# Output projection by tokens, a new order at the start of the up product, and earlier first loads of the down product

## The chip, the cores and the metric

The kernel runs on one NeuronCore of a Trainium2 chip. The metric is the device time of one execution in microseconds (us), as the median of the runs. The engines have instruction queues of their own and meet only in semaphores: TensorE (PE: matmuls and transposes), VectorE (DVE), ScalarE (ACT), GpSimd (POOL) and SyncE (SP), whose queue here issues nearly all DMAs.

## The reference, cut to what matters

```python
h = x + concat(y_attention, y_hgrn2) @ w_out        # 1024 tokens x 1024, w_out 1024 x 1024
u = rmsnorm(h, mlp_norm_w)
h = h + square(relu(u @ w_up)) @ w_down             # w_up 1024 x 4096, w_down 4096 x 1024
```

All in float32. What stands ahead of these lines (norm, input projection, neighbourhood attention, HGRN2) is not touched.

## The kernel before, in words

**Precision.** Each float32 operand is split into a rounded part (hi, by ACT or POOL) and a rest (lo, a subtraction by DVE or POOL), and each product is three matmuls: hi*hi, hi*lo, lo*hi.

**Output projection.** `w_out` comes in 8 tiles of 128 rows (tiles 32 to 39 of `TILES`), which POOL splits into a ring of 4 slots (lines 798 and 801). Two tiles make a block (`FBLK = 2`), and there are four blocks (`OUT_BLOCKS`). For each block PE computes 16 products (8 token tiles times two column halves) of 6 matmuls each (lines 2026 to 2030), DVE adds each from its bank to `resid` (line 1620), and the next block does the same again. In the last block, once both halves of a token tile are added, ACT takes the sum of squares and the inverse root (`rms`, lines 873 to 876) and DVE writes the normalised tokens (line 1295).

**Sets.** The up and down products use Strassen's scheme: 7 products in place of 8, numbered 1 to 7. For the up product the moving operand is one of 7 sets of turned (transposed) tokens, kept for the whole stage; each set has 4 parts, so there are 28 (`g`). A part is four PE transposes into a bank (`turn_set`, line 1785), a copy by ACT (hi, line 1066), and a subtraction by DVE (lo, line 1304); then its bank is free again. Sets 7 and 5 need sums of tokens that POOL makes (lines 841 and 843), set 6 four sums and set 4 four more by DVE (lines 1645 and 1649), which overwrite tokens.

**Up product.** It has 16 blocks (`UPS`, index j) of 7 products of 12 matmuls (lines 2069 to 2073). `UP_SEQ` is the order of the 112 products; those of blocks 0 and 1 are interleaved and `SET_IN` says which of them have set parts turned between their matmuls. Weight n of that order passes POOL (a sum, for products 7, 5, 6 and 3), ACT (hi, line 1076) and POOL (lo, line 834). The results are put together by DVE (`up_results`, lines 1658 to 1664, `up_last_results`), squared by ACT (`square`, lines 1099 and 1102), summed by DVE (`act_sums`) and stored to DRAM. ACT, DVE and POOL run in an order written out by hand, so each waiting instruction holds up all that follows it on its engine.

**Down product.** It has 56 slots m of 24 matmuls (lines 2100 to 2104). ACT takes the hi part of its weights (line 1113) and of its activations (line 1122); the lo parts are DVE's (line 1711) and POOL's (line 854). The first data (1 MB twice for each pair of weight tiles, and four times 0.5 MB of activations) is loaded after the stores of block 14 (`load_down`, `load_acts`), and ACT takes it in up block 15 at steps k = 3 and after.

## Time and profile before

| | |
|---|---|
| Median of 3 runs | 1390.39 us (1389.7 to 1391.82) |
| The profiled execution | 1393.67 us, span 1391.9 us |
| PE busy | 1307.8 us, 94% of the span |
| DVE, ACT, POOL busy | 875.7, 579.1, 575.5 us |
| Chain that ended last | PE 80%, DVE 10%, ACT 4% |

The span runs from the first to the last record; the execution's own time is 1.8 us longer. Times in rows are microseconds from the start of the span. A busy PE can still run at the lower of two clocks: the column PEclk is the granted share of full speed. "idle before" is the time an engine stood before an instruction, and the name behind it what ended that.

### The profile page before, as it was taken

The numbers are of one execution on the slowest core, as the hardware profiler recorded it, in microseconds if no ns is written. First come the engines' busy times: TensorE is split into PE (matmuls) and PEld (weight loads), VectorE is DVE, ScalarE is ACT, GpSimd is POOL, SyncE is SP. The second block draws the span as 40 slices with busy tenths as digits, with TensorE's granted clock in tenths as the row PEclk, the third lists the DMA queues.
The fourth block names the chain that finished last, engine by engine and source line by source line (L and its number), as shares of the span: only waits on it lengthen the run. The fifth ranks groups of instructions, "written<-read, shape, count | busy, mean of one in ns | idle before, by whom it ended". The sixth has DMA issues, their size and how long they took to land.

```text
span 1391.9 us, 18095 instructions
## 1 busy us (share of the span) xinstructions
PE 1307.8 (94%) x6624; PEld 1099.5 (79%) x6624; DVE 875.7 (63%) x1202; ACT 579.1 (42%) x1034; POOL 575.5 (41%) x324
## 2 busy tenths in 40 slices
PE   4998999999999999899986799999999999999998
PEld 4976777898888888787864688888887788888887
DVE  5445677651687786956674434344443788888885
ACT  5235656444344453232053445544443433333341
POOL 5232211123322132213246467777773544445452
PEclk9999999999999999999997899999999999999999
DMA  8341232222111010114140344454446934353433
GB/s 240 116 114 31 71 91 75 73 72 81 31 31 31 16 31 31 59 49 157 56 151 9 110 148 143 144 159 152 144 144 229 360 128 175 106 212 107 151 91 136
DMA packets 138533, 154.93 MB, mean 111 GB/s; under 512 B 11472, under 2 KB 97744, under 8 KB 138448
## 3 DMA queue, kind: packets, MB, share of 16 engines
q1 hardware_dynamic: 132976, 147.04, 32.6%
q10 hardware_dynamic: 5472, 6.75, 1.4%
q8 instruction: 54, 0.88, 0.3%
q14 instruction: 31, 0.25, 0.1%
HBM read 109.72 MB, written 44.04 MB: 110 GB/s over the span
## 4 chain that ended last, share of the span: by engine, by line
PE 80%; DVE 10%; ACT 4%; issue 3%; POOL 2%; DMA 1%; ACTq 0%; SPq 0%; DVEq 0%; POOLq 0%
PE bank L2100 7%; PE bank L2103 7%; PE bank L2104 7%; PE bank L2069 6%; PE bank L2072 6%; PE bank L2073 6%; PE bank L1820 5%; PE bank L1824 5%; PE bank L1823 5%; PE bank L1904 4%; PE bank L2026 2%; PE bank L2030 2%; PE bank L2029 2%; PE bank L1807 2%; PE bank L1810 2%
## 5 line engine op out<-in xcount | busy, mean ns | idle before, releaser
L798 POOL TENSOR_TENSOR w_hi<-stage,one_col 128x1024 fp32r<-128x1024 f32 x40 | 78.8, 1971 | 498.1 <-PE bank L1820 344.5
L854 POOL TENSOR_TENSOR a_split<-a_raw,a_split 128x1024 fp32r<-128x1024 f32 x56 | 148.1, 2663 | 170.6 <-ACT a_split L1122 170.6
L2069 PE MATMUL bank<-set,w_hi 128*128 128x512 f32 x448 | 180.7, 403 | 12.9 <-DVE u L1660 6.5
L2100 PE MATMUL bank<-w_hi,a_split 128*128 128x512 f32 x448 | 175.2, 391 | 5.4 <-issue 5.4
L2072 PE MATMUL bank<-set,w_hi 128*128 128x512 f32 x448 | 178.5, 398 | 0.0
L2073 PE MATMUL bank<-set,w_lo 128*128 128x512 f32 x448 | 178.3, 398 | 0.0
L2103 PE MATMUL bank<-w_lo,a_split 128*128 128x512 f32 x448 | 175.0, 391 | 0.0
L2104 PE MATMUL bank<-w_hi,a_split 128*128 128x512 f32 x448 | 174.9, 390 | 0.0
L1820 PE MATMUL bank<-uT_hi,w_hi 128*128 128x512 f32 x384 | 160.4, 418 | 6.4 <-DVE h_gate L1352 6.4
L1824 PE MATMUL bank<-uT_hi,w_lo 128*128 128x512 f32 x384 | 151.3, 394 | 0.0
L1823 PE MATMUL bank<-uT_lo,w_hi 128*128 128x512 f32 x384 | 150.7, 393 | 0.0
L2069 PEld LDWEIGHTS bank<-set,w_hi 128*128 128x128 f32 x448 | 85.9, 192 | 33.1 <-issue 14.3
L834 POOL TENSOR_TENSOR w_lo<-stage,w_hi 128x512 fp32r<-128x512 f32 x56 | 75.6, 1352 | 80.5 <-ACT w_hi L1076 80.5
L2100 PEld LDWEIGHTS bank<-w_hi,a_split 128*128 128x128 f32 x448 | 84.5, 189 | 23.9 <-issue 6.2
L801 POOL TENSOR_TENSOR w_lo<-stage,w_hi 128x1024 fp32r<-128x1024 f32 x40 | 101.6, 2540 | 3.1
L2073 PEld LDWEIGHTS bank<-set,w_lo 128*128 128x128 f32 x448 | 85.6, 191 | 19.7
L2072 PEld LDWEIGHTS bank<-set,w_hi 128*128 128x128 f32 x448 | 85.8, 191 | 18.6
L2104 PEld LDWEIGHTS bank<-w_hi,a_split 128*128 128x128 f32 x448 | 84.5, 189 | 17.7
L2103 PEld LDWEIGHTS bank<-w_lo,a_split 128*128 128x128 f32 x448 | 84.5, 189 | 17.4
L834 POOL TENSOR_TENSOR w_lo<-raw_b,w_hi 128x512 fp32r<-128x512 f32 x56 | 74.4, 1329 | 42.7 <-ACT w_hi L1076 42.7
L1711 DVE TENSOR_TENSOR w_lo<-raw,w_hi 128x1024 fp32r<-128x1024 f32 x35 | 74.4, 2131 | 26.4 <-ACT w_hi L1113 26.4
L1820 PEld LDWEIGHTS bank<-uT_hi,w_hi 128*128 128x128 f32 x384 | 72.9, 190 | 21.7 <-DVE h_gate L1352 7.2
(183 smaller groups left out, 2869.9 us busy)
## 6 DMA issues: line engine op xcount, KB each, us to landing
a_dram<-abuf SPq DMA_DIRECT2D x112, 256.0 KB, 2.1
a_raw<-a_dram SPq DMA_DIRECT2D x56, 512.0 KB, 3.7
stage<-in_w_in SPq DMA_DIRECT2D x32, 512.0 KB, 4.1
raw<-in_w_down SPq DMA_DIRECT2D x10, 1024.0 KB, 8.5
stage<-in_w_up SPq DMA_DIRECT2D x16, 512.0 KB, 5.0
raw_b<-in_w_up SPq DMA_DIRECT2D x16, 512.0 KB, 5.1
x_tok<-in_x SPq DMA_DIRECT2D x8, 512.0 KB, 5.5
v_dram<-vs ACTq DMA_DIRECT2D x32, 128.0 KB, 1.8
```

The costliest lines, as they stand in the source:

```text
L801: pool.tensor_tensor(w_lo[:, i, :], stage[:, i % STAGE, :], w_hi[:, i, :].bitcast(F32), ALU.subtract).then_inc(w_split, 1)
L834: pool.tensor_tensor(ring_part(w_lo, n), here, ring_part(w_hi, n).bitcast(F32), ALU.subtract).then_inc(x_lo, 1)
L854: pool.tensor_tensor(a_split[:, m % 4, 1, :], a_raw[:, m % 4, :], a_split[:, m % 4, 0, :].bitcast(F32), ALU.subtract).then_inc(b_lo, 1)
L1820: first = pe.matmul(b[:, :], w[0], u[0], start=k == 0, stop=False)
L1823: pe.matmul(b[:, :], w[0], u[1], start=False, stop=False)
L1824: ins = pe.matmul(b[:, :], w[1], u[0], start=False, stop=k == KT - 1)
L2069: first = pe.matmul(dst, w[0], u[0], start=k == 0 and p in (1, 5, 6, 7), stop=False, skip_group_check=True)
L2072: pe.matmul(dst, w[0], u[1], start=False, stop=False, skip_group_check=True)
L2073: ins = pe.matmul(dst, w[1], u[0], start=False, stop=k == 3, skip_group_check=True)
L2100: first = pe.matmul(dst, a[0], w[0], start=start, stop=False, skip_group_check=True)
L2103: pe.matmul(dst, a[0], w[1], start=False, stop=False, skip_group_check=True)
L2104: ins = pe.matmul(dst, a[1], w[0], start=False, stop=q == 1 and k == 1, skip_group_check=True)
```

## The change

- **Output projection.** Blocks 2 and 3 become one round: each of the 16 products has 12 matmuls and is added once. The split tiles 38 and 39 go to a place of their own (`w_late`), and the mixer's split parts have four places (`mixed`) in place of two. The token tiles so come to their end one after the other over the whole of the last round.
- **Start of the up product.** ACT splits weights 0 to 3 ahead of the norms, set parts 0 to 7 are turned after products 9 to 12 of the round, and (1, 6) moves ahead of (0, 4) and (0, 3). The other 20 parts are placed one by one (`TURNED_AT`), with other banks for the last two. ACT takes weights 6 to 13 in pairs between the set parts. POOL makes two sums before the last token sums. DVE takes set parts 16 to 19 between its two groups of four sums, and does the results of block 1 before the activation sums of block 0, for which one result has another place (`act_part`).
- **Start of the down product.** In SP's order the first half of the first weights and the first four activation loads come ahead of the stores of block 14, the second half after three of these stores. `a_raw` and `raw_2` change places, ACT and DVE take the first weight and ACT the first two activations earlier in block 15.

```diff
-UP_SEQ = [(0, 1), (0, 2), (1, 1), (1, 2), (0, 7), (1, 7), (0, 5), (1, 5), (0, 6), (0, 4), (0, 3), (1, 6), (1, 4), (1, 3)]
+UP_SEQ = [(0, 1), (0, 2), (1, 1), (1, 2), (0, 7), (1, 7), (0, 5), (1, 5), (0, 6), (1, 6), (0, 4), (0, 3), (1, 4), (1, 3)]
...
-SET_BANK = (4, 5, 6, 7, 4, 5, 6, 7, 1, 5, 3, 7, 1, 5, 0, 1, 5, 0, 1, 5, 0, 1, 5, 0, 5, 0, 5, 0)
-SET_IN = {(1, 1): 2, (1, 2): 3, (1, 7): 4, (0, 5): 5, (1, 5): 6}
+SET_BANK = (4, 5, 6, 7, 4, 5, 6, 7, 1, 5, 3, 7, 1, 5, 0, 1, 5, 0, 1, 5, 0, 1, 5, 0, 5, 0, 0, 1)
+TURNED_AT = {(1, 1, 2): 8, (1, 1, 3): 9, (1, 2, 0): 10, (1, 2, 1): 11, (1, 2, 2): 12, (1, 2, 3): 13, (0, 7, 0): 14,
+             (0, 7, 1): 15, (0, 7, 2): 16, (0, 7, 3): 17, (1, 7, 0): 18, (1, 7, 1): 19, (0, 5, 2): 20, (0, 5, 3): 21,
+             (1, 5, 0): 22, (1, 5, 1): 23, (0, 6, 0): 24, (0, 6, 1): 25, (1, 6, 0): 26, (1, 6, 2): 27}
...
+        mixed = [acts[:, 0], over("mixed1", [P, 2, FBLK, S], F32R, first + 49152),
+                 over("mixed2", [P, 2, FBLK, S], F32R, first + 16384), acts[:, 1]]
+        w_late = over("w_late", [P, FBLK, 2, D], F32R, first + 32768)
...
-        a_raw = over("a_raw", [P, 4, D], F32, work + 81920)
+        a_raw = over("a_raw", [P, 4, 2, D], F32, work)[:, :, :, HALF:D]
-        raw_2 = over("raw_2", [P, 4, D], F32, work)
+        raw_2 = over("raw_2", [P, 4, D], F32, work + 81920)
...
+        def act_part(j, i):
+
+            return u_tok[:, TT - 1, HALF:D] if (j, i) == (1, A22) else abuf[:, i, :]
...
-                return w_used, N_TILES - 2 if n < 4 else N_TILES
+                return w_used, N_TILES - 4 if n < 4 else N_TILES
...
-                        sp.wait_ge(down_done, 16 * (OUT_BLOCKS - 1))
+                        sp.wait_ge(down_done, 16)
...
-                        sp.wait_ge(up_used, UP_AT[(UPS - 1, 4)] + 1)
+                        sp.wait_ge(up_used, UP_AT[(UPS - 1, 5)] + 1)
...
-                    sp.wait_ge(up_used, UP_AT[(UPS - 1, 5)] + 1)
+                    sp.wait_ge(y_turned, 28)
...
-            sp.wait_ge(proj_done, len(UNITS))
...
+                if j == UPS - 2:
+                    load_down(0, (0,))
+                    for m in range(4):
+                        load_acts(m)
+                for i in (A22, A11, A12):
                     store_acts(j, i)
-            load_down(0)
+                if j == UPS - 2:
+                    load_down(0, (1,))
+                for i in (S1, S3, S2, S4):
+                    store_acts(j, i)
             load_down(1)
-            for m in range(4):
-                load_acts(m)
...
-            split_turns(1, N_TILES // RING)
+            split_turns(1, N_TILES // RING - 1)
+            for n in range(N_TILES - 4, N_TILES):
+                pool.wait_ge(w_load[n % STAGE], 16 * (n // STAGE + 1))
+                if n < N_TILES - 2:
+                    pool.wait_ge(w_used, n + 1 - RING)
+                    hi, lo = w_hi[:, n % RING, :], w_lo[:, n % RING, :]
+                else:
+                    pool.wait_ge(proj_done, len(UNITS))
+                    hi, lo = w_late[:, n % 2, 0, :], w_late[:, n % 2, 1, :]
...
+            for n in range(4):
+                up_lo(n)
+            for t in range(3):
+                token_sums(t)
+            up_sum(4)
+            up_sum(5)
+            token_sums(3)
+            up_lo(4)
+            up_lo(5)
+            for n in range(6, 7 * UPS):
+                up_sum(n)
+                up_lo(n)
...
-                    act.wait_ge(u2_done, j - 1)
+                    act.wait_ge(c22_taken, j - 1)
...
+            for n in range(4):
+                up_weights(n)
             for t in range(TT):
-                for g in {5: (0, 1), 6: range(2, KT)}.get(t, ()):
+                act.wait_ge(added, 32 + 2 * t + 2)
+                rms(1, t)
+                for g in {4: range(4), 5: range(4, 8)}.get(t, ()):
                     take_set(g)
-                act.wait_ge(added, 16 * (OUT_BLOCKS - 1) + 2 * t + 2)
-                rms(1, t)
-                if t == 3:
-                    for n in range(4):
-                        up_weights(n)
-
             keep_p1(0)
-            for n in range(4, 6):
-                up_weights(n)
+            up_weights(4)
+            up_weights(5)
             take_c11(0)
-            for g in range(8, 12):
+            take_set(8)
+            take_set(9)
+            keep_p1(1)
+            for g in range(10, 16):
                 take_set(g)
-            keep_p1(1)
-            for g in range(12, 16):
-                take_set(g)
-            for n in range(6, 12):
-                up_weights(n)
+            up_weights(6)
+            up_weights(7)
             for g in range(16, 20):
                 take_set(g)
-            up_weights(12)
+            up_weights(8)
+            up_weights(9)
             for g in range(20, 24):
                 take_set(g)
+            up_weights(10)
+            up_weights(11)
+            for g in range(24, 27):
+                take_set(g)
+            up_weights(12)
             up_weights(13)
-            for g in range(24, 28):
-                take_set(g)
+            take_set(27)
...
+            square(1, A22)
+            up_weights(17)
             square(0, A12)
-            up_weights(17)
+            up_weights(18)
             square(0, A21)
-            up_weights(18)
...
+                    if j + 1 == UPS and k == 1:
+                        down_weights(0)
+                        down_acts(0)
+                    if j + 1 == UPS and k == 2:
+                        down_acts(1)
                     if k == 3:
-                        if j + 1 == UPS:
-                            down_weights(0)
-                            down_weights(1)
                         square(j, A22)
-                        if j + 1 == UPS:
-                            down_acts(0)
-                            down_acts(1)
                     if k == 4:
                         take_c11(j)
+                        if j + 1 == UPS:
+                            down_weights(1)
...
-                    if b + 1 < OUT_BLOCKS and i == 8:
-                        mixer_lo(b + 1)
...
-                    if b == OUT_BLOCKS - 1 and i >= 3 and i % 2 and i < 2 * TT - 1:
-                        normalise_tokens(1, (i - 3) // 2)
-                    if b == OUT_BLOCKS - 1 and i >= 11:
-                        take_set(i - 11)
-            for t in range(TT - 2, TT):
-                normalise_tokens(1, t)
-            for g in range(5, 16):
+            for n in range(3 * 2 * TT):
+                i = n % (2 * TT)
...
+                if n in (8, 20, 26):
+                    mixer_lo({8: 1, 20: 2, 26: 3}[n])
...
+                if n >= 34 and i % 2 == 0:
+                    normalise_tokens(1, i // 2 - 1)
+                for g in {41: (0, 1), 42: (2, 3), 43: (4, 5), 44: (6, 7)}.get(n, ()):
+                    take_set(g)
+            normalise_tokens(1, TT - 1)
+            for g in range(8, 16):
...
+            for g in range(16, 20):
+                take_set(g)
             for t in range(4):
                 dve.wait_ge(t2_sum, t + 1)
                 high = u_tok[:, t, HALF:D]
                 dve.tensor_tensor(high, high, u_tok[:, t, 0:HALF], ALU.subtract).then_inc(t4_sum, 1)
-            for g in range(16, 28):
+            for g in range(20, 27):
...
-                if j:
+                if j >= 2:
...
+            take_set(27)
+            up_results(1)
             up_last_results(0)
             act_sums(0)
-            for j in range(1, UPS):
+            up_last_results(1)
+            act_sums(1)
+            for j in range(2, UPS):
+                if j == UPS - 1:
+                    down_weights(0)
...
+                if g == 27:
+                    pe.wait_ge(u2_done, 1)
...
-            def add_product(i, turn, place, bank0, finished, free):
+            def add_product(i, blocks, finished, free):
...
+                for b in blocks:
+                    for f in range(FBLK):
+                        a = [mixed[b][:, x_, f, P * t:P * t + P] for x_ in range(2)]
+                        if b < 3:
+                            w = [x_[:, FBLK * b % RING + f, half * HALF:half * HALF + HALF] for x_ in ring]
+                        else:
+                            w = [w_late[:, f, x_, half * HALF:half * HALF + HALF] for x_ in range(2)]
...
-            for b in range(OUT_BLOCKS):
-                pe.wait_ge(w_split, 2 * (N_IN + FBLK * (b + 1)))
-                pe.wait_ge(m_lo, FBLK * (b + 1))
+            for n, blocks in enumerate(((0,), (1,), (2, 3))):
+                pe.wait_ge(w_split, 2 * (N_IN + FBLK * (blocks[-1] + 1)))
+                pe.wait_ge(m_lo, FBLK * (blocks[-1] + 1))
                 for i in range(2 * TT):
...
-                    add_product(i, b % 2, FBLK * b % RING, 0, (1 if b == 0 else FBLK) if i == 0 else 0,
-                                max(16 * b + i - 3, 0))
-
-                    if b == OUT_BLOCKS - 1 and i >= 10:
-                        turn_set(i - 10)
-            turn_set(6)
-            turn_set(7)
+                    add_product(i, blocks, (1, FBLK, FBLK)[n] if i == 0 else 0, max(16 * n + i - 3, 0))
+                    for g in {(2, 9): (0, 1), (2, 10): (2, 3), (2, 11): (4, 5), (2, 12): (6, 7)}.get((n, i), ()):
+                        turn_set(g)
...
+                if (j, p) == (1, 6):
+                    pe.wait_ge(y_lo, 25)
...
-                    if (j, p) in SET_IN:
-                        turn_set(4 * SET_IN[(j, p)] + k)
+                    if (j, p, k) in TURNED_AT:
+                        turn_set(TURNED_AT[(j, p, k)])
```

## Rows read from the trace of the kernel before

**Rows 1.** Stretches of time: length, busy us of each engine, PEclk, DMA, GB/s
```profile
722.00:804.00 82.00, 56.56 (x256) 45.02 (x254) 41.42 (x49) 35.25 (x64) 46.19 (x35) 0.83 0.19 61
...
1060.00:1090.00 30.00, 24.63 (x100) 19.65 (x100) 13.34 (x18) 10.81 (x14) 5.32 (x3) 0.89 0.99 374
1090.00:1392.00 302.00, 297.77 (x1313) 245.94 (x1311) 249.01 (x196) 104.25 (x106) 142.82 (x54) 1.00 0.45 154
```

**Rows 2.** PE in order of time: start, length, line, operation, [idle before <- releaser]
```profile
711.97 0.66 PE L1785 MATMUL bank<-tab,u_tok 128*128 128x128 f32 x4 [1.29 <-DVE u_tok L1295]
...
722.96 0.47 PE L2069 MATMUL bank<-set,w_hi 128*128 128x512 f32 x1
...
731.08 0.77 PE L2069 MATMUL bank<-set,w_hi 128*128 128x512 f32 x1 [5.12 <-DVE set L1304]
...
742.32 0.47 PE L2069 MATMUL bank<-set,w_hi 128*128 128x512 f32 x1 [1.26 <-ACT s L1082]
...
766.12 1.09 PE L1785 MATMUL bank<-tab,u_tok 128*128 128x128 f32 x4 [12.21 <-DVE set L1304]
...
782.25 0.47 PE L2069 MATMUL bank<-set,w_hi 128*128 128x512 f32 x1 [1.59 <-DVE u L1660]
...
795.74 0.76 PE L2069 MATMUL bank<-set,w_hi 128*128 128x512 f32 x1 [4.89 <-DVE u L1660]
...
803.90 0.39 PE L2069 MATMUL bank<-set,w_hi 128*128 128x512 f32 x1
```

**Rows 3.** PE: a short wait ahead of the stage, and one set part
```profile
613.16 0.53 PE L1820 MATMUL bank<-uT_hi,w_hi 128*128 128x512 f32 x1 [2.81 <-DVE h_gate L1352]
...
737.06 0.60 PE L1785 MATMUL bank<-tab,u_tok 128*128 128x128 f32 x4
737.41 0.48 PE L2069 MATMUL bank<-set,w_hi 128*128 128x512 f32 x1
```

**Rows 4.** POOL's split of w_out tiles 36 and 38; ACT's norm of token tile 0
```profile
650.55 1.90 POOL L798 TENSOR_TENSOR w_hi<-stage,one_col 128x1024 fp32r<-128x1024 f32 x1 [20.38 <-PE bank L2026]
...
673.04 1.90 POOL L798 TENSOR_TENSOR w_hi<-stage,one_col 128x1024 fp32r<-128x1024 f32 x1 [13.76 <-PE bank L2026]
...
698.79 1.06 ACT L873 ACTIVATE u_tok<-resid 128x1024 f32<-128x1024 f32 x1 [24.01 <-DVE resid L1620]
...
700.30 0.20 ACT L876 ACTIVATE rstd<-rstd 128x1 f32<-128x1 f32 x1
```

**Rows 5.** ACT, DVE and POOL in order of time at the start of the up product
```profile
743.72 0.60 ACT L1066 ACTIVATE set<-bank 128x512 fp32r<-128x512 f32 x1 [1.54 <-PE bank L1785]
...
744.35 0.69 DVE L1304 TENSOR_TENSOR set<-bank,set 128x512 fp32r<-128x512 f32 x1 [1.94 <-ACT set L1066]
...
748.36 5.79 DVE L1645 TENSOR_TENSOR u_tok<-u_tok 128x512 f32<-128x512 f32 x4
...
762.84 1.26 POOL L829 TENSOR_TENSOR raw_b<-raw_b 128x512 f32<-128x512 f32 x1
764.84 1.27 POOL L834 TENSOR_TENSOR w_lo<-raw_b,w_hi 128x512 fp32r<-128x512 f32 x1 [0.74 <-ACT w_hi L1076]
...
790.46 0.69 DVE L1684 TENSOR_TENSOR abuf<-abuf 128x512 f32<-128x512 f32 x1 [1.65 <-ACT abuf L1102]
```

**Rows 6.** All engines in order of time where the down product begins
```profile
1077.26 1.06 ACT L1122 ACTIVATE a_split<-a_raw 128x1024 fp32r<-128x1024 f32 x1 [1.68 <-DMA a_raw<-a_dram]
1078.39 4.70 POOL L854 TENSOR_TENSOR a_split<-a_raw,a_split 128x1024 fp32r<-128x1024 f32 x2 [18.85 <-ACT a_split L1122]
1080.84 0.76 PE L2100 MATMUL bank<-w_hi,a_split 128*128 128x512 f32 x1 [5.37 <-issue]
...
1083.37 0.69 DVE L1684 TENSOR_TENSOR abuf<-abuf 128x512 f32<-128x512 f32 x1 [6.52 <-issue]
...
1086.03 1.22 DVE L1699 TENSOR_TENSOR stage<-stage 128x1024 f32<-128x1024 f32 x1
1089.37 2.49 POOL L854 TENSOR_TENSOR a_split<-a_raw,a_split 128x1024 fp32r<-128x1024 f32 x1 [6.29 <-ACT a_split L1122]
```

More of the change, by code:

```diff
@@ L335, in hybrid_block @@
         resid = place("resid", [P, TT, D], F32)
-        u3 = place("u3", [P, HALF], F32)
+        w_row = place("w_row", [P, D], F32)
         end_mlp = at[0]
@@ L346, in hybrid_block @@
         set_4 = over("set4", [P, 8, D], F32R, work)
-        w_row = over("w_row", [P, D], F32, first + 16384)
         raw_b = over("raw_b", [P, 2, D], F32, work + 32768)
@@ L1676, in act_sums @@
             def act_sums(j):
-                a = [abuf[:, i, :] for i in range(8)]
+                a = [act_part(j, i) for i in range(8)]
                 for i in (A11, A12, A21, A22):
@@ L2015, in _ @@
                         head_outputs(h)
[L2018 removed]
+            def add_product(i, blocks, finished, free):
                 t, half = divmod(i, 2)
                 pe.wait_ge(added, free)
[L2022 to L2030 removed]
+                dst = out_bank(i, 0)[:, :]
+                for b in blocks:
[5 more added lines that the diff above has]
+                            w = [w_late[:, f, x_, half * HALF:half * HALF + HALF] for x_ in range(2)]
+                        start, stop = (b, f) == (blocks[0], 0), (b, f) == (blocks[-1], FBLK - 1)
+                        first = pe.matmul(dst, a[0], w[0], start=start, stop=False)
+                        if start and finished:
+                            first.then_inc(w_used, finished)
+                        pe.matmul(dst, a[0], w[1], start=False, stop=False)
+                        ins = pe.matmul(dst, a[1], w[0], start=False, stop=stop)
```

87 lines of the change are left out of this document (39 added, 48 removed).

## The prediction

> **What bounds the kernel now.** I read the page first: PE is busy for 94% of the span and holds 80% of the chain that ended last. So nothing is to be had from the other engines' shares, only from stretches in which PE stands or runs slowly. The view of stretches then shows where these are. From 722 to 804 us PE is busy for 56.6 of 82 us at a granted clock of 0.83, and from 1060 to 1090 for 24.6 of 30 us at 0.89, while from 1090 to the end the clock is 1.00 and PE has no wait but the tail behind its last matmul [rows 1]. The change touches just these two places and the round ahead of the first.
>
> The order of time of PE, read third, gives the waits. The first up product starts at 722.96 and block 2 at 803.90, so blocks 0 and 1 take 80.9 us. The waits inside are 5.12, 1.26, 12.21, 1.59 and 4.89 us, together 25.1 [rows 2]. The work itself is 14 products of 12 matmuls and 20 set parts. The four products from 742.32 on run at about 0.235 us per matmul, thus 2.8 us per product; a set part lets the next matmul start 0.35 us later [rows 3] and costs about 0.44 with the gap behind it. That is 14 x 2.8 + 20 x 0.44 = 48.0 us. The rest, 80.9 - 48.0 - 25.1 = 7.8 us, is the clock: the matmul behind each of the three long waits takes 0.76 us and more in place of 0.47 [rows 2].
>
> The order of time of the others, read last, tells who causes the waits. The 12.21 us end with DVE's set part 16, behind ACT's copy of it, and ACT's copy stands behind six weights in a row (6 to 11). Each weight that needs a sum costs a round of POOL sum 1.26, handover and ACT copy 0.74, POOL split 1.27: 3.3 us [rows 5], in which ACT does nothing else.
>
> **Part 1, the output projection.** Before and after it is 64 x 6 matmuls, so PE's time in it stays; it has no wait but 1.29 us before the first set part [rows 2]. Block 1 starts at 650.3 (POOL's tile 36 is freed by it at 650.55) and block 2 at 672.8 [rows 4]: 22.5 us a block. In the joined round product i ends at 672.8 + 2.81 (i + 1). The new condition is that tiles 38 and 39 be split when it starts. POOL needs 4.35 us a tile; 36 and 37 go from 650.55 to 659.3, 38 to 663.6, 39 to about 668.2 with its load of 3.5 to 4 us behind the freeing of its stage. That leaves 4.6 us; cost nothing. If this cover goes, the round waits for what is missing, at most 4.35 us for a tile. The lo parts of both mixer blocks are DVE's after additions 20 and 26 and end by 667. The 16 additions saved are off PE's path.
>
> Token tile 3 is added after product 7 (695.3), its norm takes ACT 1.7 us [rows 4], its tokens are ready at about 700.3, before product 9 ends at 700.9. The 1.29 us go. The norms of tiles 4 to 6 go between the set parts; the round ends at 672.8 + 45.0 + 8 x 0.44 = 721.3. Product (0,1) starts then, 1.65 us earlier.
>
> **Part 2, blocks 0 and 1.** I walk it engine by engine. Set parts 0 to 7 are all taken at 715.9, so (0,2) waits only for ACT's copy of bank 0: (0,1) ends at 724.1, ACT ends norm 7 at 723.8, wait 0.7 in place of 5.12. (1,1) from 727.7 with parts 8 and 9; POOL's last token sums end at 728.4, just in time. (1,2) waits 1.3 for its copy, as before, and starts at 732.7; it holds parts 10 to 13, (0,7) 14 to 17, (1,7) 18 and 19.
> Part 19 needs bank 5, thus DVE's part 16. DVE ends part 15 at 740.8, then come the four sums for set 6, 5.0 to 5.8 us [rows 5], then part 16 at 746.6; PE is there at 743.6: wait 3.0. ACT is not late for it: weights 6 and 7 let it go at 744.0. From there each pair of weights is a few us ahead of its product; (1,5) waits 0 to 0.9. (1,6) waits for part 24, which ACT takes after weight 11: 0.7. Part 27 waits for the sum u2 of block 0: 0.6. (0,4) needs all 28 parts, and ACT takes the last after weight 13, which needs two more POOL rounds: ready at 768.4, PE at 765.8, wait 2.6. After that (0,4), (0,3), (1,4), (1,3) follow without a wait: u3 of block 1 is ready at 770.0, as DVE does it ahead of block 0's sums, where 4.89 us were lost. The waits sum to 0.7 + 1.3 + 3.0 + 0.5 + 0.7 + 0.6 + 2.6 = 9.4 us.
> The clock: behind a wait of 2.81 us at 613.16 nine matmuls ran at the lower level [rows 3], 9 x 0.19 = 1.7 us; behind 1.26 and 1.59 none did [rows 2]. Two of my waits are near that edge, so 0 to 3.4; I take 2.0. The stage is 48.0 + 9.4 + 2.0 = 59.4 us, handovers that I rounded 0.8 more: 60.2, and block 2 starts at 721.3 + 60.2 = 781.5, 22.4 us earlier. Can the others follow? The weight (2,1) is split by 770.3. The copy that (2,2) needs is ACT's at 789.5, behind the squares of blocks 0 and 1 and the first activation sums; PE is there at 792.7. Weight (3,1) is ready at 793.5 for 801.1. The activation sums of block 1 end near 793 and u3 of block 2 is due at 795.5. Slacks of 2 to 7 us, so nothing is lost if I am right, and each slip is paid once.
> DVE's two groups of four sums have both inputs in SBUF. With POOL at work one takes 1.45 us, with POOL standing 0.69 [rows 5]. The Trainium skill, page "SBUF — State Buffer", section "Who interferes with whom", says that a VectorE instruction with two SBUF inputs and a GpSimd instruction that reads SBUF exclude each other fully. What that would make here is rival E.
>
> **Part 3, start of the down product.** PE ends the up product at 1075.3 and waits 5.37 us for POOL's split of the first activations, which landed at 1077.2 [rows 6] in a stretch that moves 374 GB/s with the DMA engines 0.99 busy [rows 1]. Half of the weights and all four activation loads, 3 MB, now go ahead of block 14's stores, about 1045 on this clock; at 374 GB/s they are in by 1055. ACT can take weight 0 behind its copy at 1059.8 and both activations by 1063, POOL splits them by 1067, DVE weight 1 by 1074. The wait of 5.37 goes, and with it the slow matmuls behind it (eight at 0.43 for 0.23: 1.6 us); in all 7.0. What is late next is slot 2. Its chain began with the activation sums at 1083.37 and ended with POOL's split at 1091.9 [rows 6], 8.5 us. The squares now end at 1077.6, so it ends at 1086.3, and PE comes there at 1086.2; slots 3 and 4 follow with 0.5 and 0.8 us of wait. I take 1.0, bounds 0 and 3: gain 6.0. The later loads move up too, as 3 MB less are queued at 1063. Stores of block 14 behind the early loads: if one is late, DVE's results of block 15 are, worth at most the 7 us again.
>
> **Sum.** 1.65 is inside the 22.4. 22.4 + 6.0 = 28.4 us. The profiled execution took 1393.67 (span 1391.9), so it would be 1365.3; it stands 3.3 above the median 1390.39, and the median would be 1362.0.
>
> **Rivals.**
> - A: the waits move instead of going. ACT and POOL still hand each other 8 weights, now between the set parts. If each pair holds ACT until the part it delays is due, every pair costs PE one round of 3.3 us: 4 x 3.3 = 13 us more, clock losses 3 more, gain 12.4, time 1378. For it: a part's own chain is short (ACT 0.60, DVE 0.69 [rows 5]), so PE has no reserve. Against: in my walk only two pairs are met on the path. 12%.
> - B: the down start gains nothing because slot 2's chain or the DMA queue is the bound: gain 22.4 + 1, time 1367. The queue is full in that stretch [rows 1]; against it, a third of it is moved. 15%, within the forecast's own range.
> - C, slower: set parts and weights become one serial chain. If each of the 20 parts stands PE for the whole turn, copy and lo (0.4 + 0.6 + 0.7 less 0.1 of work, 1.6 us) and each of the 8 weights for 3.3, the waits are 58 us in place of 25; with slow clock all through (3 us more than now) the stage is 36 us longer, less 1.65 and 6 elsewhere: 1390.4 + 28 = 1418. It decides from a stage of 88.5 us on, 29 us above my walk. One late release in front of an in-order engine can start it; against it, banks 0, 1 and 5 turn over with at least two matmul groups between them. 5%.
> - E: each of DVE's four sums ahead of part 16 stands for a whole POOL instruction of 1.27 us first: 4 x 1.96 = 7.8 us, the wait of 3.0 becomes 5.8, time 1364.8. Against it, four took 5.79 us with POOL at work [rows 5]. 10%, inside the forecast's own range.
> - D: the change doesn't do what it says: the gains are there but blocks 2 and 3 pay them back, because the squares and sums of two blocks come at once; the slack at (2,2) is 3 us. Paid in full it would leave 1390 less 6 and some: 1384 to 1390. 5%.
>
> **How the numbers follow.** The forecast with B has 78%, A 12%, C 5%, D 5%. The forecast's own range is 1356 to 1370: below, all waits but the copies gone (9.4 + 2.0 less 2 gives 9 us, of which I allow 6); above, B and E together. The range that is asked for reaches to A, as handovers between in-order engines are easily underrated: 1354 to 1379; C, D and what lies below are left out, some 12%. About 0.2% (2.8 us) is what can be told from no change. Faster by more: 78 + 12 + 3 of D = 92%. Within it: 2%. Slower: 5 of C and 1 for what I don't see.
>
> **What would show it.** In the trace after: the wait before part 0 gone and (0,1) at about 721; the largest wait in blocks 0 and 1 about 3 us, before part 19, ended by DVE's part 16 behind its four sums; a wait of 2 to 3 us before (0,4) ended by a set part; no wait before (1,4); block 2 about 60 us behind (0,1); no wait before the first down slot and at most 1 us before slots 2 to 4. The prediction is wrong if any wait in blocks 0 and 1 is above 6 us, if the joined round waits for tile 39, or if PE waits in up blocks 2 to 15.

## The result and the profile after

| | before | after |
|---|---|---|
| Median | 1390.05 us (1389.64 to 1391.82, 4 runs) | 1370.87 us (1369.3 to 1376.59, 4 runs) |
| Ratio, 95% interval | | 0.9867 (0.9837 to 0.9897) |
| Profiled execution | 1393.67 us, span 1391.9 | 1376.59 us, span 1374.7 |

The kernel is faster by 19.2 us; forecast were 28.4, and 1362.0 us. Part of what is missing belongs to this one execution. What stands ahead of the output projection is untouched, yet its length varies: the first matmul of the projection came at 625.17 us in the profile of before, at 627.54 here, and at 620.71 and 622.57 in two further profiles of the same changed kernel. In the three profiles of the changed kernel the stages behind it differ by much less: the first one is 97.92 us in two of them, and 99.52 where slow matmuls stand behind a wait, from the first up product to the first down slot there are 335.25 to 335.39 us, and the down product takes 307.9 to 308.7. So I compare stage by stage, and put a second profile of the changed kernel (`after_third`, below) beside the first. A matmul of the up product takes PE 0.231 us (1080.84 - 5.37 - 803.90 = 271.6 us for 14 blocks of 84 [rows 2, 6]); the start of block 2 is walked back by 60 of them from the row of product (2,4).

| Stage, us | before | forecast | after | after_third |
|---|---|---|---|---|
| output projection: its first matmul to the first up product | 97.8 | 96.1 | 99.5 | 97.9 |
| blocks 0 and 1 of the up product | 80.9 | 60.2 | 61.6 | 60.1 |
| block 2 to the first down slot | 276.9 | 577.5 with the next | 273.7 | 275.3 |
| first down slot to the last matmul | 306.6 | | 307.9 | 308.0 |
| sum | 762.3 | 733.8 | 742.8 | 741.3 |

The largest term, blocks 0 and 1, came out as forecast. What is missing, 7.5 us in `after_third`, is in two others: 1.8 us in the first, the output projection (the "round" of some expectations below), and 5.8 in what lies behind the start of block 2.

Stretches of time in the changed kernel (columns as in [rows 1]): block 1 of the output projection with 11 us of block 0; blocks 0 and 1 of the up product; the start of the down product.

```profile
642.00:674.00 32.00, 29.95 (x130) 23.88 (x128) 24.99 (x25) 0.00 (x0) 19.74 (x8) 1.00 0.17 50
727.00:789.00 62.00, 52.83 (x251) 41.64 (x251) 32.44 (x39) 28.56 (x51) 40.27 (x30) 0.94 0.12 39
1048.00:1078.00 30.00, 27.42 (x119) 21.91 (x118) 19.82 (x19) 14.12 (x19) 9.70 (x5) 1.00 0.94 357
```

Blocks 0 and 1 now have PE busy for 52.8 of 62 us at a clock of 0.94, where it was 56.6 of 82 at 0.83 [rows 1]. The first line is the new loss: PE stands for 2 of 32 us in the output projection, where it had no wait, while DVE is busy for 25.

PE in order of time, its rows with a wait from there to 1100 us, answering to [rows 2] and [rows 6]:

```profile
664.27 0.50 PE L2079 MATMUL bank<-w_hi,mixed 128*128 128x512 f32 x1 [0.79 <-DVE resid L1659]
674.77 0.80 PE L2079 MATMUL bank<-w_hi,mixed 128*128 128x512 f32 x1 [2.03 <-DVE resid L1659]
...
730.73 0.47 PE L2120 MATMUL bank<-set,w_hi 128*128 128x512 f32 x1 [0.78 <-ACT s L1117]
738.59 0.47 PE L2120 MATMUL bank<-set,w_hi 128*128 128x512 f32 x1 [1.27 <-ACT s L1117]
753.40 1.09 PE L1833 MATMUL bank<-tab,u_tok 128*128 128x128 f32 x4 [3.67 <-DVE set L1343]
768.69 0.47 PE L2120 MATMUL bank<-set,w_hi 128*128 128x512 f32 x1 [0.40 <-POOL w_lo L863]
772.11 0.63 PE L1833 MATMUL bank<-tab,u_tok 128*128 128x128 f32 x4 [0.66 <-issue]
775.77 0.47 PE L2120 MATMUL bank<-set,w_hi 128*128 128x512 f32 x1 [2.35 <-issue]
...
802.83 0.47 PE L2120 MATMUL bank<-set,w_hi 128*128 128x512 f32 x1 [0.31 <-DVE s L1700]
1056.69 0.47 PE L2120 MATMUL bank<-set,w_hi 128*128 128x512 f32 x1 [1.20 <-DVE s L1700]
1074.84 0.47 PE L2151 MATMUL bank<-w_hi,a_split 128*128 128x512 f32 x1 [1.38 <-issue]
1087.52 0.47 PE L2151 MATMUL bank<-w_hi,a_split 128*128 128x512 f32 x1 [1.22 <-issue]
```

The waits of 5.12, 12.21, 4.89 and 5.37 us are gone. In blocks 0 and 1 stand 0.78, 1.27, 3.67, 0.40, 0.66 and 2.35, 9.1 us in all against 9.4 forecast, and nearly each at its place. Not forecast are the two first rows (2.8 us, in block 1 of the output projection and at its end, ended by DVE's additions), those before (2,4) and (15,4) (0.31, 1.87 in `after_third`; 1.20), and the size of the last two, before slots 2 and 4 of the down product.

### The profile page after: what moved, and what is told of

Read it like the earlier page. It is cut to its first block, busy times and chain, and to the rows that moved or that the text cites. A ratio compares the mean times of both kernels' runs of the same rounds, so it can differ in the third digit from the quotient of the medians.

```text
span 1374.7 us, 18052 instructions
## 1 busy us (share of the span) xinstructions
PE 1307.3 (95%) x6624; PEld 1096.9 (80%) x6624; DVE 870.6 (63%) x1186; ACT 578.5 (42%) x1034; POOL 578.0 (42%) x324
## 4 chain that ended last, share of the span: by engine, by line
PE 63%; POOL 11%; DVE 10%; ACT 9%; issue 5%; DMA 1%; ACTq 0%; DVEq 0%; POOLq 0%
PE bank L2151 7%; PE bank L2154 7%; PE bank L2155 7%; POOL w_lo L863 6%; PE bank L1868 5%; PE bank L1872 5%; PE bank L1871 5%; ACT w_hi L1111 5%; PE bank L1952 4%; PE bank L2079 2%; PE bank L2083 2%; PE bank L2082 2%; PE bank L1855 2%; PE bank L1790 2%; PE bank L1858 1%
## 5 line engine op out<-in xcount | busy, mean ns | idle before, releaser
L813 POOL TENSOR_TENSOR w_hi<-stage,one_col 128x1024 fp32r<-128x1024 f32 x36 | 70.9, 1971 | 466.6 <-PE bank L1868 346.9
L816 POOL TENSOR_TENSOR w_lo<-stage,w_hi 128x1024 fp32r<-128x1024 f32 x36 | 92.0, 2556 | 2.8
```

The costliest lines, as they stand in the source:

```text
L816: pool.tensor_tensor(w_lo[:, i, :], stage[:, i % STAGE, :], w_hi[:, i, :].bitcast(F32), ALU.subtract).then_inc(w_split, 1)
```

## The experiments

Times are medians; the ratio is to the kernel before on the same chip, with its 95% interval. The unchanged part ahead of the projection varies by more than most single edits move, so the effect of an edit is read from the stages of its profile. For e1, e3, e4 and e8 the intervals overlap that of the changed kernel on the same chip, and the whole times alone decide nothing. Three groups of questions: why the output projection got no shorter (e1), what the waits of the set parts are (e3, e4, e7), and why the down product's start did not show its 6 us (e2, e8, e9). e10 and e11 put the answers together.

**after_again and after_third: the changed kernel once more**, no edit, as base of its group.

> The changed kernel once more, as the base for the single edits. Its first profiled execution was 1376.6 us while three others took 1369.3 to 1371.1. Theory: the 2.4 us by which the first out-projection matmul came later there (627.54 for 625.17 us) belong to unchanged code and vary; here the time is 1369 to 1372 and the distance from the first out-projection matmul to the first up product is again 99.5 us (97.8 before), with PE waits of about 0.8 and 2.0 us ahead of the joined round. Rival: these waits were an accident of that execution; then the distance is 96 to 97 us.

> The changed kernel once more, as the base for the two others on the same chip: 1369 to 1371 us, with the round at 97.9 us, 335.3 from the first up product to the first down slot and 308.6 for the down product.

Measured: 1369.84 us (1368.81 to 1372.48), ratio 0.9848 (0.9827 to 0.9869), and 1371.12 (1370.16 to 1373.83), ratio 0.9858 (0.9839 to 0.9877). The stages are 97.92, 335.25 (first up product to first down slot) and 308.65 us, and 97.92, 335.39 and 308.01. The waits of 0.80 and 2.03 us in the projection come again in both, so they are no accident, but 99.5 us was expected and neither profile shows it. The difference is the clock: behind the wait of 2.03 us the first matmul takes 0.80 us in the first profile and 0.50 in these two.

**e1_mixer_early: VectorE's mixer parts ahead of GpSimd's splits.**

```diff
-                if n in (8, 20, 26):
-                    mixer_lo({8: 1, 20: 2, 26: 3}[n])
+                if n in (8, 11, 14):
+                    mixer_lo({8: 1, 11: 2, 14: 3}[n])
```

> Changed kernel, but DVE makes the lo parts of mixer blocks 2 and 3 after additions 11 and 14 of the first out-projection block, where POOL has nothing to do, in place of after 20 and 26, where POOL splits tiles 36 to 39. Theory (DVE's two-input subtraction and POOL's split exclude each other): the two subtractions of a block go from 4.9 and 6.2 us back to 2.4 us, the waits of 0.8 and 2.0 us and the slow matmuls behind them go, the up product starts 3 to 4 us earlier counted from the first out-projection matmul (96.1 us), and the time falls by 3 to 4 us against the changed kernel. Rival (the subtractions are slow because of their new places in memory, or DVE has too much to do in any case): they stay at 4.9 us or more and the time does not move by more than 1 us.

Measured: 1368.78 us (1366.13 to 1369.88), ratio 0.9827 (0.981 to 0.9845); the output projection takes 94.50 us in place of 97.92, and both waits are gone. The median is only 1.1 us lower than in `after_again`. First DVE and POOL of the changed kernel in order of time, where the mixer's lo parts are made (the last two rows of DVE are the pair above them, one by one):

```profile
642.00 2.36 DVE L1564 TENSOR_TENSOR mixed<-na_back,mixed 128x1024 fp32r<-128x1024 f32 x2
...
658.69 4.93 DVE L1564 TENSOR_TENSOR mixed<-h_v,mixed 128x1024 fp32r<-128x1024 f32 x2
...
667.94 6.18 DVE L1564 TENSOR_TENSOR acts<-h_v,acts 128x1024 fp32r<-128x1024 f32 x2
667.94 2.85 DVE L1564 TENSOR_TENSOR acts<-h_v,acts 128x1024 fp32r<-128x1024 f32 x1
670.71 3.40 DVE L1564 TENSOR_TENSOR acts<-h_v,acts 128x1024 fp32r<-128x1024 f32 x1
```

```profile
654.96 2.40 POOL L841 TENSOR_TENSOR w_lo<-stage,w_hi 128x1024 fp32r<-128x1024 f32 x1
...
659.28 3.25 POOL L841 TENSOR_TENSOR w_lo<-stage,w_hi 128x1024 fp32r<-128x1024 f32 x1
662.50 2.87 POOL L838 TENSOR_TENSOR w_late<-stage,one_col 128x1024 fp32r<-128x1024 f32 x1
...
667.82 1.89 POOL L838 TENSOR_TENSOR w_late<-stage,one_col 128x1024 fp32r<-128x1024 f32 x1
669.79 3.25 POOL L841 TENSOR_TENSOR w_late<-stage,w_late 128x1024 fp32r<-128x1024 f32 x1
```

and DVE of e1, with POOL idle until 651.05:

```profile
644.36 2.35 DVE L1564 TENSOR_TENSOR mixed<-h_v,mixed 128x1024 fp32r<-128x1024 f32 x2
...
648.50 2.35 DVE L1564 TENSOR_TENSOR acts<-h_v,acts 128x1024 fp32r<-128x1024 f32 x2
```

The same pair of subtractions takes 2.35 us with POOL idle and 4.93 or 6.18 beside it, while POOL's own 2.40 and 1.90 become 3.25 and 2.87. The additions queued behind them come late. PE can be four banks ahead, which is four products or 5.6 us (22.5 us a block of 16), and DVE's 6.18 us and the additions due by then are more. In e1 all three pairs take 2.35 us in the places in memory that they have in the changed kernel, so those places are not the cause. The Trainium skill's rule that forecast E rests on (page "SBUF — State Buffer", "Who interferes with whom") names just this pair: a VectorE instruction with two SBUF inputs and a GpSimd instruction that reads SBUF; the one that comes second stands until the first has ended. The trace agrees. Alone, one subtraction takes 1.18 us (half of 2.35). POOL's instruction ends at 669.71 (667.82 + 1.89), and 1.18 later would be 670.89; DVE's first ends at 670.79. POOL's next would end 2.40 behind that, at 673.19, and ends at 673.04; DVE's second would end 1.18 behind that, at 674.22, and ends at 674.11. So the two take turns, each standing for the rest of the other's instruction.

**e3_weights_6_7: two weights between the set parts.**

```diff
-            for g in range(10, 16):
-                take_set(g)
+            take_set(10)
+            take_set(11)
             up_weights(6)
+            take_set(12)
+            take_set(13)
             up_weights(7)
+            take_set(14)
+            take_set(15)
```

> Changed kernel, but ACT takes weight 6 between set parts 11 and 12 and weight 7 between 13 and 14, in place of both after part 15. POOL, which stood for 7.9 us there, then makes its splits and sums before DVE's four sums for set 6. Theory (the wait of 3.7 us before set part 19 is those four sums, slowed from 0.7 to 1.44 us each by POOL): the four sums take about 3 us, the wait falls to about 1 us, time 2.5 to 3 us less (up to 4 with the clock). Rival (the sums take 1.44 us each whatever POOL does): the wait stays at 3.5 us or so, time within 1 us.

Measured: 1368.68 us (1366.63 to 1369.69), ratio 0.9829 (0.9812 to 0.9846). The wait of 3.67 before part 19 becomes 1.51, with a new one of 0.89 before part 23, and the stretch from the first up product to the first down slot 332.74 us for 335.3. DVE's four sums ahead of part 16, in the changed kernel, then in e3:

```profile
746.90 5.75 DVE L1682 TENSOR_TENSOR u_tok<-u_tok 128x512 f32<-128x512 f32 x4
```

```profile
742.86 3.25 DVE L1686 TENSOR_TENSOR u_tok<-u_tok 128x512 f32<-128x512 f32 x4
```

In e3 POOL stands from 743.8 to 748.7, and the four sums take 3.25 us. So 2.2 of the 3.67 us were the sums standing for POOL, which the forecast had inside its 5.0 to 5.8 us for four. Not all of the gain is this: the two waits are together 1.3 us shorter, and the weights, taken earlier, also bring product (2,4) forward, 73.2 us behind the first up product in place of 75.9 (see e4), with a wait of 0.32 for 1.87.

**e4_part27_early: the last set part ahead of weight 13.**

```diff
             up_weights(12)
-            up_weights(13)
             take_set(27)
+            up_weights(13)
```

> Changed kernel, but ACT takes set part 27 ahead of weight 13 in place of behind it. Theory: the wait of 2.3 us before (0,4) is ACT standing for POOL's sum for weight 13; it falls to about 0.7 us. But by the trace PE then meets DVE's sum u3 of block 2 before (2,4), which the same ACT and POOL chain sets, and where it already waits 1.9 us; so the time moves by less than 1 us. Rival (every wait removed in blocks 0 and 1 is time gained): 1.6 us less from the first up product to the first down slot.

Measured: 1371.3 us (1370.84 to 1373.34), ratio 0.9857 (0.9835 to 0.9879): no gain. The wait before (0,4) falls from 2.35 to 0.77 us, and the time comes back. PE of e4:

```profile
768.86 0.48 PE L2120 MATMUL bank<-set,w_hi 128*128 128x512 f32 x1 [0.77 <-issue]
791.86 0.47 PE L2120 MATMUL bank<-set,w_hi 128*128 128x512 f32 x1 [0.52 <-ACT s L1117]
797.56 0.47 PE L2120 MATMUL bank<-set,w_hi 128*128 128x512 f32 x1 [2.69 <-POOL w_lo L863]
```

and of `after_third`, with DVE in front of the same product:

```profile
796.35 0.47 PE L2120 MATMUL bank<-set,w_hi 128*128 128x512 f32 x1 [1.87 <-POOL w_lo L863]
```

```profile
790.19 0.69 DVE L1725 TENSOR_TENSOR abuf<-abuf,u_tok 128x512 f32<-128x512 f32 x1 [3.69 <-ACT abuf L1137]
...
791.52 1.67 DVE L1728 TENSOR_TENSOR abuf<-u_tok,abuf 128x512 f32<-128x512 f32 x1
793.22 1.66 DVE L1730 TENSOR_TENSOR abuf<-abuf 128x512 f32<-128x512 f32 x1
794.81 0.67 DVE L1697 TENSOR_TENSOR u<-s,bank 128x512 f32<-128x512 f32 x1
795.52 0.69 DVE L1700 TENSOR_TENSOR s<-u,bank 128x512 f32<-128x512 f32 x1
```

The row names POOL, but product (2,4) starts right behind DVE's second result of block 2 (795.52 + 0.69). That stands behind the activation sums of block 1, which wait for ACT's last square of block 1 until 790.19, and two of which take 1.67 us beside POOL. Counted from the first up product, (2,4) starts after 75.8 us in the changed kernel, 75.9 in `after_third`, e4 and e8, whatever the waits in between. It is the next bound, and nothing won ahead of it counts unless ACT and POOL come early too, as in e3.

**e7_before_order: the kernel before, with ACT's weights placed between set parts.**

```diff
-            for n in range(6, 12):
-                up_weights(n)
+            up_weights(6)
+            up_weights(7)
             for g in range(16, 20):
                 take_set(g)
-            up_weights(12)
+            up_weights(8)
             for g in range(20, 24):
                 take_set(g)
-            up_weights(13)
+            up_weights(9)
+            up_weights(10)
             for g in range(24, 28):
                 take_set(g)
+            up_weights(11)
+            up_weights(12)
+            up_weights(13)
```

> Kernel BEFORE with one edit in ACT's order: the set parts 16 to 19 are taken after weights 6 and 7, 20 to 23 after weight 8, 24 to 27 after 9 and 10, in place of six weights in a row ahead of part 16. Theory (the wait of 12.2 us is those weights): DVE's eight sums become the bound, they end at 759.7, so the wait before part 19 falls to 6 to 7 us and the time by 4 to 6 us. Rival (POOL's splits are what the products need, the order only moves the wait): the waits of blocks 0 and 1 still sum to 25 us, time unchanged.

Measured: 1392.09 us (1389.59 to 1396.62, 12 runs), ratio 1.0008 (0.9994 to 1.0021): no gain, and the theory's 4 to 6 us are wrong. The waits of blocks 0 and 1 are 25.8 us in sum, as the rival had it (25). PE of e7:

```profile
755.52 1.09 PE L1789 MATMUL bank<-tab,u_tok 128*128 128x128 f32 x4 [4.47 <-DVE set L1308]
768.86 0.63 PE L1789 MATMUL bank<-tab,u_tok 128*128 128x128 f32 x4 [2.77 <-DVE set L1308]
774.98 0.47 PE L2073 MATMUL bank<-set,w_hi 128*128 128x512 f32 x1 [1.60 <-DVE u L1664]
794.16 0.76 PE L2073 MATMUL bank<-set,w_hi 128*128 128x512 f32 x1 [10.57 <-DVE u L1664]
```

The 12.21 us become 4.47 and 2.77, and the 4.89 before (1,4) become 10.57: DVE makes that result behind block 0's activation sums, and stands for 7.33 us before them until ACT's squares are done at 788.9. So ACT's order alone is worth nothing. The other half alone, DVE's results of block 1 first, was not run.

**e2_down_undone: part 3 of the change taken back** (SP's order, ACT's and DVE's).

```diff
-                if j == UPS - 2:
-                    load_down(0, (0,))
-                    for m in range(4):
-                        load_acts(m)
...
+            load_down(0)
             load_down(1)
+            for m in range(4):
+                load_acts(m)
...
                     if k == 3:
+                        if j + 1 == UPS:
+                            down_weights(0)
+                            down_weights(1)
                         square(j, A22)
+                        if j + 1 == UPS:
+                            down_acts(0)
+                            down_acts(1)
...
```

> Changed kernel with the third part undone: first down-product loads after the stores of block 14, ACT and DVE take them in the order of before. My prediction's term for this part was 6.0 us; by the trace after, the wait of 5.4 us and 1.6 us of slow clock were traded for waits of 1.2, 1.4 and 1.2 us, so by that reading the part is worth 3.2 us. Expect 3 us slower than the changed kernel, with one PE wait of about 5.4 us before the first down slot. Rival (the loads were hidden anyway, the part is worth nothing): within 1 us of the changed kernel. Rival (6.0 us as predicted): 6 us slower.

Measured: 1377.69 us (1375.57 to 1379.94), ratio 0.99 (0.9881 to 0.9919). It is 7.9 us slower than `after_again`, 6.2 by the stages (343.54 + 306.61 against 335.25 + 308.65). I expected 3 us from the waits in the trace after, and the rival of 6.0, the prediction's own term, is what came. But this is no proof of the term: the wait that the part removes is now larger than in the kernel before, 9.44 us, and what it leaves is larger too, 4.6 us of waits in `after_again` where 1.0 was forecast. ACT's copies of the first bank in blocks 14 and 15, in the kernel before:

```profile
1039.83 0.58 ACT L1082 ACTIVATE s<-bank 128x512 f32<-128x512 f32 x1
1059.25 0.58 ACT L1082 ACTIVATE s<-bank 128x512 f32<-128x512 f32 x1
```

the same two in e2, and e2's first down slot:

```profile
1023.02 0.58 ACT L1112 ACTIVATE s<-bank 128x512 f32<-128x512 f32 x1
1042.43 0.58 ACT L1112 ACTIVATE s<-bank 128x512 f32<-128x512 f32 x1
...
1064.13 0.77 PE L2144 MATMUL bank<-w_hi,a_split 128*128 128x512 f32 x1 [9.44 <-issue]
```

ACT's period is 19.41 to 19.42 us a block in both. PE's is 271.6 / 14 = 19.40. ACT is not busy all this time, nor is POOL. They hand each other the weights, POOL a sum, ACT the hi part, POOL the lo part, and each stands for the other in between. One block of the kernel before (columns as in [rows 1]) and two handovers in it:

```profile
1000.00:1019.40 19.40, 19.40 (x86) 15.79 (x85) 8.06 (x9) 9.14 (x17) 14.62 (x12) 1.00 0.46 149
...
1005.45 0.63 ACT L1076 ACTIVATE w_hi<-raw_b 128x512 fp32r<-128x512 f32 x1 [3.35 <-POOL raw_b L823]
1006.16 1.29 POOL L834 TENSOR_TENSOR w_lo<-raw_b,w_hi 128x512 fp32r<-128x512 f32 x1 [0.74 <-ACT w_hi L1076]
```

So this is a second chain, and it has the same pace as PE: what PE wins over it in blocks 0 and 1 it keeps as a lead, and ACT and POOL don't catch up. From ACT's last copy to PE's end of the up product there are 16.2 us in the kernel before (1080.84 - 5.37 - 1059.25) and 12.3 in e2 (1064.13 - 9.44 - 1042.43). To the first down slot there are 21.6 and 21.7: that slot goes by this chain (the stores of block 14, the loads behind them, the splits), and PE's 4 us of lead end in its wait, 9.44 for 5.37.

**e8_keep_dve and e9_keep_dve_down_undone: a shorter chain on ACT.** From block 2 on DVE copies the first bank in ACT's place; e9 takes part 3 back as well.

```diff
                 square(j - 1, A21)
-                keep_p1(j)
...
+            def keep_p1(j):
+                dve.wait_ge(up_done, UP_AT[(j, 1)] + 1)
+                dve.wait_ge(c22_taken, j - 1)
+                dve.tensor_copy(s1[:, j % 2, :], bank[4 * (j % 2)][:, :]).then_inc(p1_kept, 1)
...
                 up_last_results(j)
+                if j + 1 < UPS:
+                    keep_p1(j + 1)
                 act_sums(j)
```

> Changed kernel, but the copy of bank 0 that product 2 of a block needs is made by DVE instead of ACT in blocks 2 to 15 (ahead of the activation sums of the block before, where DVE stands for 6.7 us). Theory (ACT and POOL hand each other the weights in a chain that takes 19.42 us a block, while PE needs 19.39, so the 4 us that PE gained on them in blocks 0 and 1 is never made up and comes due where the down product begins): with 0.5 to 0.6 us less per block on ACT the chain catches up, ACT is again 16 us ahead of the end of the up product at its last block instead of 12 to 13.5, the PE waits of about 1.2, 2.1 and 1.2 us around the start of the down product shrink to 1 us or less in sum, time 3 to 4 us less than the changed kernel (1369.8). Rival (those waits come from the DMA queue or from DVE's own work at that place): they stay, time within 1 us.

> The same edit together with the third part undone. With the third part undone alone PE waited 9.4 us before the first down slot, where the kernel before had 5.4. Theory: the difference of 4 us is the lag of ACT and DVE behind PE, so with the lag healed the wait is 5.4 to 6 us again and the time about 4 us less than with the third part undone alone (1377.7), thus 1373 to 1374. Rival (the new places of the buffers or the later release of one make the late loads worse): the wait stays at 9.4 us and the time at 1377.

Measured: e8 1367.27 us (1366.12 to 1369.17), ratio 0.9826 (0.9807 to 0.9845); e9 1372.62 (1371.59 to 1374.2), ratio 0.9864 (0.9842 to 0.9886). PE around the start of the down product, e8 and then e9:

```profile
1048.58 0.47 PE L2127 MATMUL bank<-set,w_hi 128*128 128x512 f32 x1 [0.84 <-DVE s L1699]
1065.78 0.47 PE L2158 MATMUL bank<-w_hi,a_split 128*128 128x512 f32 x1 [0.43 <-issue]
```

```profile
1059.54 0.77 PE L2151 MATMUL bank<-w_hi,a_split 128*128 128x512 f32 x1 [6.82 <-issue]
1083.37 0.47 PE L2151 MATMUL bank<-w_hi,a_split 128*128 128x512 f32 x1 [0.32 <-issue]
```

ACT's copies for C11 (`take_c11`, one a block) in e9:

```profile
1012.66 0.58 ACT L1122 ACTIVATE abuf<-bank 128x512 f32<-128x512 f32 x1
1031.83 0.58 ACT L1122 ACTIVATE abuf<-bank 128x512 f32<-128x512 f32 x1
```

In e8 the last three waits shrink from 3.9 us (1.21, 1.47, 1.22 in `after_third`) to 1.3, that before (2,4) from 1.87 to 0.38, the down product from 308.0 to 306.2, and e9's wait is 6.82 where e2's was 9.44. By the stages e8 gains 2.5 us, less than the 3 to 4 expected. The lead explains the size: the copy of 0.58 us leaves ACT, but a block of the chain gets shorter by 0.2 us only, 19.2 for 19.42, and POOL is busy for 15.1 us a block where it was 14.6 (why is not traced). Over the 12 blocks from 2 to 14 that is 2.6 us, just what e9's wait lost. So e9 does not come down to the 5.4 to 6 that I expected: a part of the lead stays.

The wait of 1.2 us before (15,4) has a cause of its own, and the change made it. DVE of `after_third`, with the subtraction for down weight 0 that Part 3 moved ahead of block 15's results:

```profile
1045.30 3.43 DVE L1752 TENSOR_TENSOR w_lo<-stage,w_hi 128x1024 fp32r<-128x1024 f32 x1
```

The same subtraction takes 1.23 us when POOL stands (at 1055.34, down weight 1); here POOL splits the first activations from 1044.91 on. It looks like the case of e1 once more; that this subtraction makes the wait is shown by e11, which moves it behind the results.

**e10_mixer_weights_keep: e1, e3 and e8 together. e11_and_down_weight: and DVE's weight 0 later.**

```diff
-                if j == UPS - 1:
-                    down_weights(0)
                 up_results(j)
                 if j == UPS - 1:
+                    down_weights(0)
                     down_weights(1)
```

> The changed kernel with three edits together: VectorE makes the mixer's lo parts for blocks 2 and 3 after additions 11 and 14, ScalarE takes weight 6 behind part 11 and weight 7 behind part 13, and VectorE keeps P1 of blocks 2 and on. Theory (three separate causes: the round's waits, the wait ahead of part 19, the pace of ScalarE and GpSimd in blocks 2 to 15): the stage terms add up. Round 94.5 us (from 97.9), first up product to first down slot about 332 (334.7 with the keep alone, less the 2.5 of the weights), down product 306.2; against the changed kernel on the same chip 3.4 + 3.2 + 2.5 = 9 us less, about 1361. Rival (what is won early is paid back later, as by the part placed earlier, or at VectorE's u3 of block 2): the sum stays at the keep's own gain or a little over, 1365 to 1367, and the waits before (2,4) or before the first down slot are 2 to 5 us longer than with the keep alone.

> The three edits and a fourth: VectorE takes down weight 0 behind the results of block 15, and not ahead of them. Theory (VectorE's subtraction for down weight 0, 3.4 us beside GpSimd's work, delays the results of block 15 and so makes PE's wait of 0.8 to 1.2 us in that block): this wait goes and nothing comes in its place, 0.8 to 1.2 us less than the three edits alone, about 1360. Rival (the lo part of weight 0 is needed for the first down slot as soon as that begins): the wait in block 15 goes, and one of 1 us or more stands before the first down slot; no difference in time.

Measured: e10 1361.73 us (1360.68 to 1367.03), ratio 0.9799 (0.9778 to 0.9821); e11 1363.11 (1359.65 to 1364.86), ratio 0.9788 (0.9769 to 0.9807). The stages of e10 are 94.50, 331.98 and 306.11 us, in sum 732.6, 8.7 less than `after_third` where 9 were expected: the terms add up (3.4, 2.6 and 2.5), and the interval is clear of that of `after_third`. e10 is faster than both kernels. In e11 the wait of 0.77 in block 15 goes, that before slot 2 becomes 0.67 for 0.38, and one of 1.21 comes before slot 4; the stages sum to 732.7 and the intervals overlap: no difference, as its rival had it, though the waits are not before the first slot, where the rival put them. PE of e11 there:

```profile
1063.11 0.47 PE L2161 MATMUL bank<-w_hi,a_split 128*128 128x512 f32 x1 [0.67 <-issue]
1075.79 0.47 PE L2161 MATMUL bank<-w_hi,a_split 128*128 128x512 f32 x1 [1.21 <-issue]
```

## Why the prediction was right in the middle and wrong at both ends

- **Faster, within the range:** right. 1370.87 lies in 1354 to 1379, but just outside the likeliest case's own range of 1356 to 1370, and 9 of the forecast 28.4 us did not come. The range took them in because it reached out to rival A, which did not occur. (The chance of "faster", 78 + 12 + 3, is 93 and not 92%.)
- **Part 2, blocks 0 and 1, the walk:** right. 60.2 forecast, 60.1 and 61.6 measured; the waits 9.1 for 9.4; the 3.0 before part 19 was 3.67, the 2.6 before (0,4) 2.35, and no wait before (1,4). The clock term of 2.0 was a guess between 0 and 3.4, and two profiles with the same waits differ in it: the granted clock is 0.94 in the first and 0.97 in `after_third`, with 1.5 us between the stages.
- **Part 1, "cost nothing":** wrong, by 1.8 us at full clock (97.9 for 96.1), 3.4 in the profiled execution. I asked only whether POOL would have tile 39 in time. It had. I had noted that DVE's lo parts for the mixer end by 667, and priced them as if POOL stood. They took 4.93 and 6.18 us in place of 2.36 and ended at 674.1 (671.7 on the clock of before), and their cost fell on block 1, ahead of the round that I had looked at (e1). The exclusion that I weighed for the four sums in rival E acts here as well, and there I did not look.
- **Part 1, the gain of 1.65:** it is real, hidden by this. With e1's edit the output projection takes 94.5 us, 3.3 less than before, so the waits cost 3.4 us, and a gain that I had not counted hides half of that. The uncounted 1.6 us lie in the matmuls: the second block (96 matmuls) takes 21.76 us in e1 and 22.50 before, the rest 0.9 less beyond the two waits of 1.29 and 0.36 that go. Why a matmul is shorter there is not shown.
- **"Nothing is lost" behind block 2:** wrong, and this is the step that failed most. That PE waits in blocks 2 to 15 was one of my signs of being wrong, and it does, before (2,4) and (15,4). The slack before (2,4) was to be 2.5 us; DVE's result is late by 1.9, as ACT's last square of block 1 and two sums of 1.67 us are. This is what rival D described, at less than a tenth of its price. And I took it that ACT follows PE's earlier start all the way. Its chain with POOL has no reserve to do so in blocks 2 to 15 (e2, e9). Of the 5.8 us that are missing behind the start of block 2, these waits are 1.9 and 1.2, and those before slots 2 and 4 are 1.7 more than forecast; the last 1.0 is not traced.
- **Part 3, 6.0 us:** the edit is worth 6.2 (e2), but that this is near 6.0 is luck: the term was read from the wait of 5.37 in the trace before, Part 2 makes that wait 9.44, and what is left behind the edit is larger by about as much. As a term of the sum it was wrong. What PE won over the chain of ACT and POOL was lost again for the most part where the down product begins. Block 2 to the last matmul: 583.5 before, 583.3 in `after_third` and 581.6 in the first profile, 577.5 forecast.
- **Residual waits of 1.0 at slots 2 to 4:** 2.6 and 2.7, and 3.4 in `after_again`, so at and above the upper bound of 3, and not the 1.0 that I took; slot 2's chain is where it was looked for.
- **Rivals:** A and C are out, since no wait in blocks 0 and 1 is over 3.7 us. B's time is near the measured one, but for another reason: the edit does gain. E's wait of 5.8 is not seen, four sums took 5.75 us as in the trace before. Its mechanism is what happens all the same: three of the four take 1.75 to 1.79 us and one about 0.7, as POOL stood for ACT while it ran, and E had all four at 1.96.

## What to carry to other kernels

Two terms read from the same trace add up only if the second wait is still set by the same thing once the first is gone: ask whose chain sets each, and whether that chain moves with the gain. When PE and a chain of other engines have the same period a block, a lead that one wins is kept to the next place where they meet, and an edit on that chain is worth what it takes off the period, not the length of the instruction that it moves. And when a change puts one engine's work into another stretch, look what the neighbours do there, not only how long it takes where it was.

## What was not expected of the hardware

- A pair of DVE subtractions with both inputs in SBUF (128x1024) takes 2.35 us with POOL idle, 4.93 and 6.18 beside POOL's; POOL's instructions are up to 1.5 times as long (2.87 for 1.90). The rows fit two engines that take turns, instruction by instruction. DVE's additions with one input in PSUM take 0.69 us beside POOL as without it.
- The unchanged part ahead of the output projection took from 620.7 to 627.5 us in profiles of kernels that are the same up to there, more than the smaller effects of this study; the stages behind it repeat within 0.8 us where no slow matmuls are in them. The cause was not looked for.
